# Three-pass products with whole passes, an input projection on raw rows, and branch rows split one per tile

## The chip, the cores and the metric

The kernel runs on one core of a Trainium2 chip. A core has TensorE (PE: matrix products into PSUM banks), VectorE (DVE), ScalarE (ACT), GpSimd (POOL) and SyncE (SP, which mostly issues DMAs). Each engine runs its own list of instructions in order; they wait for one another by semaphores. The metric is the device time of one execution in microseconds, as the median of several runs.

## The reference

One layer of a streaming encoder over T = 1152 tokens (1024 of a prompt and 8 x 16 of samples), width D = 1024. A combined projection of the normalised input feeds three token mixers and their gates; the gated branches are merged and projected, and cross attention and a gated convolutional feed-forward block follow:

```python
def rmsnorm(x, g):
    y = x * rsqrt(mean(x * x, axis=-1) + 1e-6)
    return y * g
...
xn = rmsnorm(x, norm_mix)
lru_x, lru_y, swa, rw, gl = split(xn @ w_in)          # 1024 -> 52 x 128 columns
oA = rg_lru(causal_conv(lru_x)) * gelu(lru_y)
oB = sliding_window_attention(swa)                    # window 128, learned sinks
oC = rwkv7_mix(rw)                                    # token shift, delta rule
gates = sigmoid(gl + b_gate)                          # 3 x 1024
merged = sum(gates[n] * (o @ w_branch[n]) for n, o in enumerate((oA, oB, oC)))
x = x + merged @ w_out
x = x + cross_attention(rmsnorm(x, norm_x), mem_keys, mem_values)
x = x + conv_ffn(rmsnorm(x, norm_ffn))
y = rmsnorm(x, norm_final)
```

The mean of squares is one number per token, so `rmsnorm(x, g) @ W` is also `((x * g) @ W) * rs` with `rs` = 1 / root of the mean square of each token.

## The kernel before

Activations lie transposed: 128 features on the partitions, k = 8 blocks of features, 1152 tokens along the free axis in 3 chunks of 384. The program is a chain of stages with a barrier after each: input projection (`stage_in_projection`, L584), linear recurrence, delta rule, merge (`stage_merge`, L1745, which also computes memory keys and values and the queries), cross attention, and a tail (output of the attention, feed-forward).

Nearly all matmuls belong to a `Product` (L116): y = W x in float32 accuracy from rounded factors. ScalarE rounds a weight tile of 128 output columns, `hi` (`split_hi`, L168), VectorE takes the remainder, `lo` = raw - hi (`split_lo`, L177), and x is split into `xh` and `xl` in the same way. TensorE adds three passes, hi xh, lo xh and hi xl, into one PSUM bank per chunk. Weight tiles alternate between two sets of buffers (s = 0, 1), two tiles are a pair p, and `load_first` and `load_rest` (L143, L149) let SP load a raw tile as soon as its predecessor in the buffer has its remainder taken. `pipeline` (L187) writes out the order on ScalarE and VectorE: the split of a tile, then the evacuation `evac` of the tile before it. `products` (L238) writes out TensorE's: `first_tile` (L262) follows the operands as they come, `tile` (L242) the rest. In `tile`, the three passes are done for k-block 0, then for k-block 1, and so on; ahead of the first matmul stand a wait for `rest` (the remainder of this weight) and one for `used` (the banks evacuated). The function `extra` puts other work, that of the window attention, behind every ninth matmul of sixteen tiles of the input projection.

The input projection first normalises: SP loads the constants (135 KB), the masks (1060 KB), then x in three chunks of columns (1536 KB each), the first two weight tiles behind the first chunk. `Norm` (L311) squares on ScalarE (L343), sums over features by matmuls with a matrix of ones (L366), takes the root on ScalarE (L350) and the reciprocal on VectorE (L373), and then the normalised x is split (up to L390). Of 52 tiles the first 14 are stored as they are, the next 14 are shifted and mixed by VectorE, and the last 24 are gates. ScalarE copies a tile from PSUM (L688) and issues its store; the shifted tiles it copies into padded rows. `PromptWindows` puts the attention within windows beside 16 of the tiles (scores, softmax on VectorE from L542 to L578, transposes on TensorE at L480).

In the merge stage each of the three branches has 4 rows (128 x 1152) as operands and 8 tiles of weights with 4 k-blocks. A `StreamSplit` (L1703) loads rows into a ring of three, rounds them on ScalarE (L1728) and takes the remainder on VectorE (L1732). ScalarE and VectorE do the four rows of branch n + 1 as a block ahead of the pipeline of branch n, with gates (L1851) and splits of weights behind them.

Of the kernel before, what the change touches and what calls it, by code (L numbers as in the profile page):

```python
# [14 lines left out]
F32 = mybir.dt.float32  # L15
F32R = mybir.dt.float32r
ALU = mybir.AluOpType
# [98 lines left out]
class Product:  # L116
# [121 lines left out]
    def products(self, pe, x_rest, by_chunk, beside=None, freed=None, after_row=None, after_tile=None):  # L238
# [3 lines left out]
        def tile(p, s, wait, extra=None, freed=None):  # L242
            pe.wait_ge(self.rest, p * 2 + (s + 1))
            if wait:
                pe.wait_ge(self.used, (p * 2 + (s - 1)) * self.ntc)
            elif self.after:
                pe.wait_ge(self.after.used, 2 * self.after.pairs * self.after.ntc)
            passes = ((self.hi, self.xh), (self.lo, self.xh), (self.hi, self.xl))
            for k in range(self.kt):
                for n, (w, x) in enumerate(passes):  # L250
                    for c in range(self.ntc):
                        last = k == self.kt - 1 and n == 2
                        mm = pe.matmul(self.bank[s][c][:, 0:self.tc], w[s][:, k, :],  # L253
                                       x[:, k, c * self.tc:(c + 1) * self.tc], start=(k == 0 and n == 0), stop=last)
                        if last:
                            mm.then_inc(self.ready, 1)
                if extra:
                    extra(pe, p, s, k)
                if freed and k < self.kt - 1:
                    mm.then_inc(freed, 1)  # L260
# [18 lines left out]
        first_tile()  # L279
        tile(0, 1, False)  # L280
# [303 lines left out]
def stage_in_projection(nc, env, io):  # L584

    with Stage(nc, "inproj") as st:
# [5 lines left out]
        x_in = [st.sem(f"x_arrived{c}") for c in range(NTC)]  # L592
# [5 lines left out]
        norm = Norm(st, "norm", xt, vec[:, VAT["norm_mix"]:], xh, xl, env["mask"]("ones"), banks)  # L598
        norm.eps = env["eps"]
# [12 lines left out]
        with nc.Block() as block:  # L612
            @block.sync
            def _(sp):
                sp.dma_start(vec[:], io["vec"]).then_inc(vec_in, 16)
                sp.dma_start(masks[:], io["masks"]).then_inc(vec_in, 16)
                for c in range(NTC):
                    sp.dma_start(xt[:, :, c * TC:(c + 1) * TC], io["xt"][:, :, c * TC:(c + 1) * TC]).then_inc(x_in[c], 16)
                    if c == 0:
                        prod.load_first(sp)  # L620
# [12 lines left out]
            def _(pool):  # L633
# [3 lines left out]
                pool.wait_ge(norm.rest, NTC * KD)  # L637
# [20 lines left out]
            def _(act):  # L658
                act.wait_ge(eps_set, 2)
                norm.squares(act, x_in, prod)  # L660
                norm.roots(act)

                def shifted(p, s):
                    if after_first(p):
                        act.wait_ge(S(f"shifted{s}"), p * 2 - 2 * R0)
                        act.wait_ge(S(f"z_last{s}"), p - R0)
                        act.wait_ge(S(f"z_last_prompt{s}"), p - R0)
                    else:
                        act.wait_ge(norm.rest, NTC * KD)
                    for c in range(NTC):  # L670
                        act.wait_ge(prod.ready, (p * 2 + s) * NTC + (c + 1))
                        n = TC if c < NTC - 1 else SEQ - c * TC
                        act.copy(zp[s][:, 1 + c * TC:1 + c * TC + n], prod.bank[s][c][:, 0:n]).then_inc(S(f"z_copied{s}"), 1)
                    act.copy(padded(zp[s])[:, :, 1:], prod.bank[s][NTC - 1][:, TC - NB * NS:TC].rearrange("p (b s) -> p b s", b=NB)).then_inc(S(f"z_copied{s}"), 1)
                    act.wait_ge(S(f"z_copied{s}"), p * 4 + (4 - 4 * R0))
                    act.sem_inc(prod.used, NTC)
# [2030 lines left out]
```

## Time and profile before

| | before |
|---|---|
| runs (us) | 2826.38, 2832.47, 2825.57; median 2826.38 |
| profiled execution | 2832.27 us, span 2830.7 us |
| mean granted TensorE clock | 0.949 |
| TensorE busy | 2559.3 us, 90% of the span, 20320 matmuls |
| VectorE busy | 1344.4 us, 47% |
| ScalarE busy | 729.4 us, 26% |
| GpSimd busy | 226.9 us, 8% |
| DMA | 258.92 MB, mean 91 GB/s |

Shares are of the span. An engine's busy time says nothing on what waits for what: that is in the chain of work that ended last and in the table of waits. Times in the rows further down are microseconds from the start of the span.

### The profile page before, as it was taken

The numbers are of one execution on the slowest core, as the hardware profiler recorded it, in microseconds if no ns is written. First come the engines' busy times: TensorE is split into PE (matmuls) and PEld (weight loads), VectorE is DVE, ScalarE is ACT, GpSimd is POOL, SyncE is SP. The second block draws the span as 40 slices with busy tenths as digits, with TensorE's granted clock in tenths as the row PEclk, the third lists the DMA queues.
The fourth block names the chain that finished last, engine by engine and source line by source line (L and its number), as shares of the span: only waits on it lengthen the run. The fifth ranks groups of instructions, "written<-read, shape, count | busy, mean of one in ns | idle before, by whom it ended". The sixth has DMA issues, their size and how long they took to land. (4 is left out here: it accounts for less than half of the span.)

```text
span 2830.7 us, 48844 instructions
## 1 busy us (share of the span) xinstructions
PE 2559.3 (90%) x20320; PEld 2447.7 (86%) x20320; DVE 1344.4 (47%) x2030; ACT 729.4 (26%) x1085; POOL 226.9 (8%) x382
## 2 busy tenths in 40 slices
PE   6999999999657888948999996699999999999996
PEld 4999999999546777838999895599999999999995
DVE  5012334341466777533663513436665555643346
ACT  4111222221344444313332302323111111112122
POOL 0001110000212233200000000000000000000000
PEclk9999999999858999959999998999999999999998
DMA  3222233322630110024441417421111111132233
GB/s 131 82 91 82 91 107 110 108 92 90 138 116 28 33 36 20 14 82 166 141 152 63 147 72 276 142 94 38 45 54 69 57 59 69 69 107 98 72 94 123
DMA packets 138020, 258.92 MB, mean 91 GB/s; under 512 B 43440, under 2 KB 86240, under 8 KB 135056
## 3 DMA queue, kind: packets, MB, share of 16 engines
q1 hardware_dynamic: 103104, 184.25, 20.1%
q0 software_dynamic: 10464, 43.52, 4.5%
q10 hardware_dynamic: 24320, 29.23, 2.9%
q8 instruction: 102, 1.67, 0.3%
q14 instruction: 30, 0.25, 0.0%
HBM read 190.36 MB, written 67.52 MB: 91 GB/s over the span
## 5 line engine op out<-in xcount | busy, mean ns | idle before, releaser
L253 PE MATMUL tail_bank<-tail_x_hi,tail_w_hi 128*128 128x384 f32 x1494 | 359.6, 339 | 8.2 <-DVE tail_w_lo L180 8.2
L253 PE MATMUL tail_bank<-tail_x_lo,tail_w_hi 128*128 128x384 f32 x1494 | 358.3, 339 | 0.0
L253 PE MATMUL tail_bank<-tail_x_hi,tail_w_lo 128*128 128x384 f32 x1494 | 358.2, 339 | 0.0
L253 PE MATMUL inproj_bank<-inproj_xh,inproj_win_hi 128*128 128x384 f32 x1224 | 283.0, 340 | 0.0
L253 PEld LDWEIGHTS tail_bank<-tail_x_hi,tail_w_hi 128*128 128x128 f32 x1494 | 270.7, 188 | 11.8 <-DVE tail_w_lo L180 11.3
L253 PE MATMUL inproj_bank<-inproj_xl,inproj_win_hi 128*128 128x384 f32 x1224 | 278.6, 336 | 0.0
L253 PE MATMUL inproj_bank<-inproj_xh,inproj_win_lo 128*128 128x384 f32 x1224 | 278.5, 336 | 0.0
L253 PEld LDWEIGHTS tail_bank<-tail_x_hi,tail_w_lo 128*128 128x128 f32 x1494 | 270.9, 188 | 0.0
L253 PEld LDWEIGHTS tail_bank<-tail_x_lo,tail_w_hi 128*128 128x128 f32 x1494 | 270.7, 188 | 0.0
L253 PEld LDWEIGHTS inproj_bank<-inproj_xh,inproj_win_hi 128*128 128x128 f32 x1224 | 216.2, 189 | 2.7 <-issue 2.7
L253 PEld LDWEIGHTS inproj_bank<-inproj_xh,inproj_win_lo 128*128 128x128 f32 x1224 | 218.1, 188 | 0.0
L253 PEld LDWEIGHTS inproj_bank<-inproj_xl,inproj_win_hi 128*128 128x128 f32 x1224 | 218.1, 188 | 0.0
L175 ACT CAST tail_w_hi<-tail_w_raw 128x1024 fp32r<-128x1024 f32 (+2 forms) x100 | 92.5, 925 | 474.9 <-PE tail_bank L253 314.0
L253 PE MATMUL merge_bank<-merge_operands,merge_w_hi 128*128 128x384 f32 x840 | 181.9, 340 | 13.5 <-DVE merge_w_lo L180 13.5
L180 DVE TENSOR_TENSOR inproj_win_lo<-inproj_win_raw,inproj_win_hi 128x1024 fp32r<-128x1024 f32 x52 | 63.5, 1223 | 250.0 <-ACT inproj_win_hi L175 250.0
L253 PEld LDWEIGHTS merge_bank<-merge_operands,merge_w_hi 128*128 128x128 f32 x840 | 151.7, 192 | 14.2 <-DVE xt L1932 8.9
L2503 DVE TENSOR_TENSOR tail_room<-tail_bank,tail_rs 128x384 f32<-128x384 f32 x132 | 59.5, 506 | 181.8 <-PE tail_bank L253 181.5
L253 PE MATMUL merge_bank<-merge_operands,merge_w_lo 128*128 128x384 f32 x588 | 135.4, 338 | 0.0
L180 DVE TENSOR_TENSOR tail_w_lo<-tail_w_raw,tail_w_hi 128x1024 fp32r<-128x1024 f32 (+2 forms) x100 | 106.8, 1068 | 54.8 <-ACT tail_w_hi L175 54.7
L1741 DVE TENSOR_TENSOR xt<-tail_bank,xt 128x384 f32<-128x384 f32 x96 | 47.9, 551 | 168.5 <-PE tail_bank L253 155.9
L253 PEld LDWEIGHTS merge_bank<-merge_operands,merge_w_lo 128*128 128x128 f32 x588 | 106.5, 191 | 0.0
L688 ACT COPY inproj_z<-inproj_bank 128x384 f32<-128x384 f32 x114 | 47.6, 497 | 201.9 <-PE inproj_bank L253 201.2
(388 smaller groups left out, 3935.3 us busy)
## 6 DMA issues: line engine op xcount, KB each, us to landing
inproj_win_raw<-in_w_in SPq DMA_DIRECT2D x52, 512.0 KB, 3.6
tail_w_raw<-in_w_up SPq DMA_DIRECT2D x44, 512.0 KB, 4.3
scratch_z<-inproj_z ACTq DMA_DIRECT2D x38, 576.0 KB, 2.8
merge_gate<-scratch_z POOLq DMA_DIRECT2D x24, 576.0 KB, 4.0
scratch_h<-tail_room SPq DMA_DIRECT2D x18, 576.0 KB, 3.1
tail_room<-scratch_h POOLq DMA_DIRECT2D x18, 576.0 KB, 4.6
tail_w_raw<-in_w_down SPq DMA_DIRECT2D x24, 384.0 KB, 3.1
merge_w_raw<-in_w_mem_kv SPq DMA_DIRECT2D x16, 512.0 KB, 3.4
```

The source lines that it names most:

```text
L175: act.copy(self.hi[s][:, 0:self.kt], self.raw[s][:, 0:self.kt]).then_inc(self.rounded, 1)
L180: dve.tensor_tensor(self.lo[s][:, 0:self.kt], self.raw[s][:, 0:self.kt], self.hi[s][:, 0:self.kt].bitcast(F32), ALU.subtract).then_inc(sel ...
L253: mm = pe.matmul(self.bank[s][c][:, 0:self.tc], w[s][:, k, :], x[:, k, c * self.tc:(c + 1) * self.tc], start=(k == 0 and n == 0), stop=last)
L688: act.copy(out[s][:, c * TC:(c + 1) * TC], prod.bank[s][c][:, 0:TC]).then_inc(prod.used, 1)
L1741: dve.tensor_tensor(row, prod.bank[s][c][:, 0:TC], row, ALU.add).then_inc(prod.used, 1)
L2503: dve.tensor_tensor(u[s][:, 2 + c * TC:2 + c * TC + n], up.bank[s][c][:, 0:n], rs[:, c * TC:c * TC + n], ALU.mult).then_inc(S(f"u{s}"), 1)
```

## The change

Three edits, all without a change in what is computed.

1. `tile` does each pass for all k-blocks before the next pass, in the order hi xh, hi xl, lo xh. At its start it waits for `rounded` (the `hi` of this weight); for `rest` (the `lo`) it waits ahead of the first matmul of the third pass. Where rows of x are to be freed one by one (`freed`), the order stays by k-block. The other work (`extra`) still comes behind every ninth matmul.
2. The input projection works on raw x times the gain. x is loaded by rows, w0, x0, w1, x1 to x7, and the masks behind them. ScalarE makes xh (L698 of the new kernel) and squares (L693), VectorE xl (L748) and the sum of squares (L743). TensorE does the first two tiles together, row by row (`first_pair`, L296), then three matmuls with ones on the summed squares (L811). The first two outputs are copied unscaled and multiplied by `rs` in SBUF; of all later tiles VectorE multiplies the banks by `rs` as it evacuates them (L775), and ScalarE only issues the store. `put_sinks` comes behind the first pair.
3. In the merge stage the rows of branches 1 and 2 are handled one per tile of the branch before: in gate i ScalarE issues the load of row i and rounds row i - 1, and VectorE takes the remainder of row i - 1 behind evacuation i.

On TensorE, a tile of the input projection in its first loop stood before as a sequence of threes (`inproj_xh`, `inproj_xl`: the split x; `inproj_win_hi`, `inproj_win_lo`: the split weight tile), twenty-four threes in a tile:

```order
L253 MATMUL inproj_bank<-inproj_xh,inproj_win_hi 128x384 [waits inproj_win_w_rest]
L253 MATMUL inproj_bank<-inproj_xh,inproj_win_hi 128x384 x2
L253 MATMUL inproj_bank<-inproj_xh,inproj_win_lo 128x384 x3
L253 MATMUL inproj_bank<-inproj_xl,inproj_win_hi 128x384 x3
L253 MATMUL inproj_bank<-inproj_xh,inproj_win_hi 128x384 x3
```

and in the changed kernel such a tile, whole, is this (its wait for the rounded weight, `w_rounded`, stands on an instruction ahead of it that only handles the loop's numbers):

```order
L245 ISA [waits inproj_win_w_rounded]
L258 MATMUL inproj_bank<-inproj_xh,inproj_win_hi 128x384 [waits inproj_win_product_used]
L258 MATMUL inproj_bank<-inproj_xh,inproj_win_hi 128x384 x23
L258 MATMUL inproj_bank<-inproj_xl,inproj_win_hi 128x384 x24
L258 MATMUL inproj_bank<-inproj_xh,inproj_win_lo 128x384 [waits inproj_win_w_rest]
L258 MATMUL inproj_bank<-inproj_xh,inproj_win_lo 128x384 x23
```

The wait for the remainder has moved from the first matmul to the forty-ninth, and it is carried by that matmul.

On ScalarE, at the start of the merge stage, the difference reads thus (`merge_operands_9069` and `merge_operands_8918` are the operands of branch 0, `merge_operands` those of branch 1, `merge_branch` the ring of raw rows, L1816 of the new kernel the rounding of a row, L1804 the issue of its load):

```order
 L175 CAST merge_w_hi<-merge_w_raw 128x512 x2
-L1728 CAST merge_operands_9069<-merge_branch 128x1152 x4
-L1728 CAST merge_operands<-merge_branch 128x1152 x4
-L1851 ACT_TABLE_LOAD
-L1851 ACTIVATE merge_gate<-merge_gate,vec 128x1152
-L175 CAST merge_w_hi<-merge_w_raw 128x512
```

```order
+L1816 CAST merge_operands_8918<-merge_branch 128x1152 x4
+L1929 ACT_TABLE_LOAD
+L1929 ACTIVATE merge_gate<-merge_gate,vec 128x1152
+L1804 DMA merge_branch<-scratch_branch 128x1152
+L175 CAST merge_w_hi<-merge_w_raw 128x512
+L1929 ACTIVATE merge_gate<-merge_gate,vec 128x1152
+L1816 CAST merge_operands<-merge_branch 128x1152
+L1804 DMA merge_branch<-scratch_branch 128x1152
+L175 CAST merge_w_hi<-merge_w_raw 128x512
```

Of the eight roundings ahead of the first gate four are left; the others stand one behind each gate, each followed by the issue of the next load.

The diff, cut to its core:

```diff
@@ products
         def tile(p, s, wait, extra=None, freed=None):
-            pe.wait_ge(self.rest, p * 2 + (s + 1))
+            pe.wait_ge(self.rounded, p * 2 + (s + 1))
...
-            passes = ((self.hi, self.xh), (self.lo, self.xh), (self.hi, self.xl))
-            for k in range(self.kt):
-                for n, (w, x) in enumerate(passes):
+            passes = ((self.hi, self.xh), (self.hi, self.xl), (self.lo, self.xh))
+            if freed:
+                steps = [(n, k) for k in range(self.kt) for n in range(3)]
+            else:
+                steps = [(n, k) for n in range(3) for k in range(self.kt)]
+            for i, (n, k) in enumerate(steps):
+                if (n, k) == (2, 0):
+                    pe.wait_ge(self.rest, p * 2 + (s + 1))
...
+        def first_pair():
+            passes = ((self.hi, self.xh), (self.lo, self.xh), (self.hi, self.xl))
+            for k in range(self.kt):
+                pe.wait_ge(x_rest, k + 1)
+                for s in range(2):
+                    if k == 0:
+                        pe.wait_ge(self.rest, s + 1)
...
@@ stage_in_projection, SyncE
-                sp.dma_start(masks[:], io["masks"]).then_inc(vec_in, 16)
-                for c in range(NTC):
-                    sp.dma_start(xt[:, :, c * TC:(c + 1) * TC], io["xt"][:, :, c * TC:(c + 1) * TC]).then_inc(x_in[c], 16)
-                    if c == 0:
-                        prod.load_first(sp)
+                for k in range(KD):
+                    if k < 2:
+                        sp.dma_start(prod.raw[k][:], prod.w(0, k)).then_inc(prod.arrived[k], 16)
+                    sp.dma_start(xt[:, k], io["xt"][:, k]).then_inc(x_in[k], 16)
+                sp.dma_start(masks[:], io["masks"]).then_inc(S("masks_in"), 16)
@@ ScalarE
+                for k in range(KD):
+                    if k < 2:
+                        prod.split_hi(act, 0, k)
+                    act.wait_ge(x_in[k], 16)
+                    act.activation(xh[:, k], xt[:, k], ACT.Identity, scale=gain(k)).then_inc(S("x_rounded"), 1)
+                    if k:
+                        square(k - 1)
+                square(KD - 1)
...
+                def first_pair():
+                    act.wait_ge(S("row_summed"), KD - 1)
+                    for s in range(2):
+                        for c in range(NTC):
+                            act.wait_ge(prod.ready, s * NTC + c + 1)
+                            act.copy(out[s][:, chunk(c)], prod.bank[s][c][:, 0:TC]).then_inc(prod.used, 1)
+                        if s:
+                            break
+                        for c in range(NTC):
+                            act.wait_ge(S("summed"), c + 1)
+                            act.activation(rs[:, chunk(c)], sum_bank(c), ACT.Sqrt, scale=1.0 / D, bias=env["eps"][:, 0:1]).then_inc(S("rooted"), 1)
...
-                    for c in range(NTC):
-                        act.wait_ge(prod.ready, (p * 2 + s) * NTC + (c + 1))
-                        act.copy(out[s][:, c * TC:(c + 1) * TC], prod.bank[s][c][:, 0:TC]).then_inc(prod.used, 1)
                     act.wait_ge(prod.used, (p * 2 + (s + 1)) * NTC)
-                    act.dma_start(io["z"][bass.ds(p * 2 + s, 1)].rearrange("o p t -> (o p) t"), out[s][:]).then_inc(stored[s], 16)
+                    store(p, s)
@@ VectorE
+                        for c in range(NTC):
+                            dve.wait_ge(prod.ready, (p * 2 + s) * NTC + (c + 1))
+                            dve.tensor_tensor(out[s][:, chunk(c)], prod.bank[s][c][:, 0:TC], rs[:, chunk(c)], ALU.mult).then_inc(prod.used, 1)
@@ TensorE
+                def sums():
+                    pe.wait_ge(S("masks_in"), 16)
+                    pe.wait_ge(S("row_summed"), KD - 1)
+                    for c in range(NTC):
+                        if c >= 2:
+                            pe.wait_ge(S("rooted"), c - 1)
+                        pe.matmul(sum_bank(c), env["mask"]("ones"), acc[:, chunk(c)], start=True, stop=True).then_inc(S("summed"), 1)
+                prod.products(pe, S("x_rest"), False, windows, after_pair=sums)
@@ stage_merge, ScalarE
-                    if n < 2:
-                        splits[n + 1].scalar(act)
...
+                        if n < 2:
+                            next_row(splits[n + 1], p * 2 + s)
+                    def next_row(stream, i):
+                        if i == 0:
+                            act.wait_ge(splits[n].rest, KM)
+                            if n:
+                                act.wait_ge(prods[0].ready, KD * NTC)
+                        if 1 <= i <= KM:
+                            stream.scalar_row(act, i - 1)
+                        if i < KM:
+                            stream.load_row(act, i)
@@ VectorE
-                    if n < 2:
-                        splits[n + 1].vector(dve)
...
+                        if n < 2 and 1 <= p * 2 + s <= KM:
+                            splits[n + 1].vector_row(dve, p * 2 + (s - 1))
```

## Rows read from the trace of the kernel before

**Rows 1.** The chain that ended last: start, length, engine, tile, line, count

```profile
1962.46 544.56 PE tail_bank L253 x3094
```

**Rows 2.** Waits of TensorE: waiting line, releaser, total us, times, longest

```profile
PE merge_bank L253 <- DVE merge_w_lo L180: 20.3, 4, 8.6
...
PE tail_bank L253 <- DVE tail_w_lo L180: 14.2, 8, 4.5
...
PE inproj_bank L366 <- ACT inproj_norm_sq L343: 13.7, 3, 13.1
...
PE inproj_bank L273 <- DVE inproj_xl L390: 11.2, 15, 2.8
```

**Rows 3.** Timeline of the start: time, length, engine, line, operation, [wait before]

```profile
11.11 1.28 ACT L343 ACT_TABLE_LOAD   x1 [11.11 <-DMA inproj_xt<-in_xt]
...
23.71 1.28 ACT L350 ACT_TABLE_LOAD   x1
25.01 0.58 ACT L350 ACTIVATE inproj_norm_rs<-inproj_bank,eps 128x384 f32<-128x384 f32 x1
...
64.03 0.68 PE L253 MATMUL inproj_bank<-inproj_xh,inproj_win_hi 128*128 128x384 f32 x3
...
76.52 0.68 PE L253 MATMUL inproj_bank<-inproj_xh,inproj_win_hi 128*128 128x384 f32 x3
```

**Rows 4.** DMA from 0 to 100 us, 40 slices of 2.5 us

```profile
GB/s 29 314 366 405 419 398 401 402 206 272 26 0 0 0 0 0 0 3 0 0 7 3 0 0 0 0 236 129 80 0 0 230 96 126 0 0 236 56 154 0
```

**Rows 5.** Timeline of the merge stage: instructions of 1152 columns

```profile
1543.52 1.17 ACT L1872 ACTIVATE merge_gate<-xt 128x1152 f32<-128x1152 f32 x1
...
1550.58 1.26 ACT L1878 ACTIVATE merge_operands<-xt,vec 128x1152 fp32r<-128x1152 f32 x1
...
1543.40 1.35 DVE L1963 TENSOR_TENSOR merge_branch<-merge_branch,merge_gate 128x1152 f32<-128x1152 f32 x1
...
1552.26 1.41 DVE L1967 SCALAR_TENSOR_TENSOR merge_merged_lo<-xt,vec,merge_operands 128x1152 fp32r<-128x1152 f32 x1
```

**Rows 6.** Timeline of a window tile: ScalarE, VectorE, TensorE

```profile
430.09 1.26 ACT L688 COPY inproj_z<-inproj_bank 128x384 f32<-128x384 f32 x3
...
432.08 1.05 ACT L175 CAST inproj_win_hi<-inproj_win_raw 128x1024 fp32r<-128x1024 f32 x1 [0.72 <-ACT inproj_z L688]
...
431.82 0.49 DVE L542 COPY inproj_attended<-inproj_bank 128x128 f32<-128x128 f32 x2 [6.86 <-PE inproj_bank L459]
433.16 1.22 DVE L180 TENSOR_TENSOR inproj_win_lo<-inproj_win_raw,inproj_win_hi 128x1024 fp32r<-128x1024 f32 x1 [0.85 <-ACT inproj_win_hi L175]
...
438.91 0.69 DVE L578 TENSOR_TENSOR inproj_scores<-inproj_scores,inproj_stat 128x512 f32<-128x512 f32 x1
...
443.56 0.60 PE L480 MATMUL inproj_bank<-masks,inproj_scores 128*128 128x128 f32 x4
```

**Rows 7.** Busy time (PE, PEld, DVE, ACT, POOL), granted clock, DMA share, GB/s of a stretch

```profile
1294.00:1300.30 6.30, 6.17 (x21) 6.18 (x22) 1.99 (x4) 1.31 (x2) 1.05 (x2) 0.57 0.78 264
```

**Rows 8.** Timeline at the memory keys: VectorE's reciprocals, TensorE's wait

```profile
1563.38 7.37 DVE L1991 RECIPROCAL merge_gated<-merge_gated 128x384 f32<-128x384 f32 x3
...
1571.88 0.58 PE L253 MATMUL merge_bank<-merge_mem_hi,merge_w_hi 128*128 128x256 f32 x1 [5.94 <-DVE merge_w_lo L180]
```

**Rows 9.** The page's groups: busy us, mean ns, idle before and releaser

```profile
L2503 DVE TENSOR_TENSOR tail_room<-tail_bank,tail_rs 128x384 f32<-128x384 f32 x132 | 59.5, 506 | 181.8 <-PE tail_bank L253 181.5
...
L180 DVE TENSOR_TENSOR tail_w_lo<-tail_w_raw,tail_w_hi 128x1024 fp32r<-128x1024 f32 (+2 forms) x100 | 106.8, 1068 | 54.8 <-ACT tail_w_hi L175 54.7
```

**Rows 10.** Timeline of the merge stage: TensorE's stalls, ScalarE's rows

```profile
1294.13 1.33 PE L253 MATMUL merge_bank<-merge_operands,merge_w_hi 128*128 128x384 f32 x3 [8.62 <-DVE merge_w_lo L180]
...
1351.70 1.32 PE L253 MATMUL merge_bank<-merge_operands,merge_w_hi 128*128 128x384 f32 x3 [4.91 <-DVE merge_w_lo L180]
...
1281.80 1.16 ACT L1728 CAST merge_operands<-merge_branch 128x1152 fp32r<-128x1152 f32 x1 [5.82 <-DMA merge_branch<-scratch_branch]
...
1303.12 0.62 ACT L175 CAST merge_w_hi<-merge_w_raw 128x512 fp32r<-128x512 f32 x1 [3.27 <-PE merge_bank L253]
```

More of the change, by code:

```diff
@@ L247, in tile @@
                 pe.wait_ge(self.after.used, 2 * self.after.pairs * self.after.ntc)
-            passes = ((self.hi, self.xh), (self.lo, self.xh), (self.hi, self.xl))
-            for k in range(self.kt):
-                for n, (w, x) in enumerate(passes):
[L251 to L260, printed above, removed]
+            passes = ((self.hi, self.xh), (self.hi, self.xl), (self.lo, self.xh))
[6 more added lines that the diff above has]
+                    pe.wait_ge(self.rest, p * 2 + (s + 1))
+                w, x = passes[n]
+                for c in range(self.ntc):
+                    mm = pe.matmul(self.bank[s][c][:, 0:self.tc], w[s][:, k, :],
+                                   x[:, k, c * self.tc:(c + 1) * self.tc], start=(i == 0), stop=(i == len(steps) - 1))
+                    if i == len(steps) - 1:
+                        mm.then_inc(self.ready, 1)
+                if i % 3 == 2:
+                    if extra:
+                        extra(pe, p, s, i // 3)
+                    if freed and k < self.kt - 1:
+                        mm.then_inc(freed, 1)
         def first_tile():
@@ L278, in first_tile @@
                     after_row(k)
-        first_tile()
-        tile(0, 1, False)
+        def first_pair():
[5 more added lines that the diff above has]
+                        pe.wait_ge(self.rest, s + 1)
+                    for n, (w, x) in enumerate(passes):
+                        for c in range(self.ntc):
+                            last = k == self.kt - 1 and n == 2
+                            mm = pe.matmul(self.bank[s][c][:, 0:self.tc], w[s][:, k, :],
+                                           x[:, k, c * self.tc:(c + 1) * self.tc], start=(k == 0 and n == 0), stop=last)
+                            if last:
+                                mm.then_inc(self.ready, 1)
+        if after_pair:
+            first_pair()
+            after_pair()
+        else:
+            first_tile()
+            tile(0, 1, False)
         if after_tile:
@@ L597, in stage_in_projection @@
         vec, masks = env["vec"], env["masks"]
[L598 to L599 removed]
+        gain = lambda k: vec[:, VAT["norm_mix"] + k:VAT["norm_mix"] + k + 1]
+        chunk = lambda c: slice(c * TC, (c + 1) * TC)
+        sum_bank = lambda c: banks[6 + c % 2][:, 0:TC]
         prod = Product(st, "win", KD, Z_N // 2, wtile(io["w_in"], KD), xh, xl, banks)
@@ L686, in evac @@
-                    for c in range(NTC):
-                        act.wait_ge(prod.ready, (p * 2 + s) * NTC + (c + 1))
-                        act.copy(out[s][:, c * TC:(c + 1) * TC], prod.bank[s][c][:, 0:TC]).then_inc(prod.used, 1)
+                    if isinstance(p, int) and p == 0:
+                        first_pair()
+                        return
+                    if isinstance(p, int) and p == 1 and s == 0:
+                        for i in range(2):
+                            act.wait_ge(S("first_scaled"), i + 1)
+                            store(0, i)
@@ L1786, in _ @@
                         splits[0].load(sp)
-                    if n < 2:
-                        if n:
-                            sp.wait_ge(prods[0].ready, KD * NTC)
-                        sp.wait_ge(splits[n].rest, KM)
-                        splits[n + 1].load(sp)
                     prods[n].load_rest(sp)
```

107 lines of the change are left out of this document (66 added, 41 removed).

## The prediction

> **What bounds the kernel now.** I read the page's first section first: TensorE is busy for 90% of the span and no other engine for half of it. The chain of waits then shows whether that is one dense stretch, and it is: one row of it is 3094 matmuls in 544.56 us without a gap, 0.176 us each [rows 1]. There are tile boundaries inside that row, and the tiles before the change take two waits at their start, so a wait whose semaphore is already up costs nothing that the trace shows. In such stretches the change can't gain, since the matmuls keep their number (20,320 less 24 ones-matmuls plus 3). What it can gain stands in the table of what TensorE waits for [rows 2]: 20.3 us before tiles of the merge stage and 14.2 us before tiles of the tail for a weight remainder (`w_lo`), 13.7 us for squares and 11.2 us for rows of `xl` at the start of the input projection. The wait for the very first operands of the merge stage stays as it is: the four rows of branch 0 are still loaded and split as a block, ahead of everything.
>
> **The start, before.** The timeline of the first 80 us [rows 3]: the first chunk of x is there at 11.11, squares, ones-matmuls on them, a first root at 25.01, reciprocals and the normalisation follow, and the first two tiles are done when tile (1,0) starts at 76.52. A tile in full flow is the 12.49 us from 64.03 to 76.52, for 72 matmuls: 0.1735 us each.
>
> **The start, after.** Eight rows of x (576 KB each) come instead of three chunks (1536 KB), and masks (1060 KB) move behind all of them. The slices of 2.5 us in [rows 4] give what had been moved by when: 2731 KB (2.797 MB) ahead of the end of the first chunk are through at 10.0, and it was used at 11.1, so 1.1 us lie between. By the same slices 647 KB (constants, w0) are through at 4.4 and 1223 KB (and x0) at 6.1: w0 is there at 5.5, x0 at 7.2. Then ScalarE multiplies row 0 (1.26, [rows 5]) to 8.5, VectorE takes the remainder (1.41) to 9.9, and TensorE starts at about 10; I take 10.5. The two tiles are 144 matmuls, 144 x 0.1735 = 25.0 us. Is TensorE what bounds them? Per row it needs 18 x 0.1735 = 3.1 us, ScalarE 1.26 + 1.17 = 2.43 (product and square), VectorE 1.41 + 1.35 = 2.76 (remainder and sum), a row of x 576 KB at about 400 GB/s = 1.5 us. So yes, narrowly. For a low clock after the idle start I add 2.5 us, which is what the restart in the merge stage cost (below), at a granted clock of 0.57; the pair then ends at 38. Behind it stand three ones-matmuls, and the third waits for the first root: tile (0,0) is ready 1.6 us before the pair's end; ScalarE then does one weight split (about 1.05), three evacuations (1.26, both [rows 6]), the table load (1.28) and a root (0.58) [rows 3], 4.2 us, so the third ones-matmul starts 2.6 after the pair's end and is through in some 0.5. Tile (1,0) starts at about 42 (41 by the terms, one for the hand-overs): 76.5 - 42 = **34.5 us gained**. Bounds: with the clock up at once 37; with VectorE as the bound and a low clock for the whole pair (6.17 / 21 = 0.294 us a matmul, [rows 7], 42 us) 18. The reciprocals (7.4 us for three, [rows 8]) and the scaling of the first two outputs lie beside tile (1,0) and wait on no one there.
>
> The table load is in the trace 1.28 us, and the root starts 0.02 us behind it [rows 3]. The Trainium skill ("ScalarE: Activation LUTs", section "What ACT_TABLE_LOAD costs") gives a switch 1283 ns of load and some 1380 ns of drain. By that page tile (1,0) would start 1.4 us later and the sum be 1.4 us smaller; the row shows no such drain, and I take the row.
>
> **Other tiles of the projection.** Their evacuation goes from ScalarE copies to VectorE products (0.506 us a chunk for such an instruction, [rows 9]), ScalarE only issues the store once VectorE is done. Outside the window tiles a tile leaves 12.5 us for 1.5 us of evacuation, 1.22 of split and the mixing, so TensorE covers it: 0. In the sixteen window tiles VectorE also has the softmax. In [rows 6] ScalarE ends its evacuation at 431.35, issues the store and begins the split 0.72 us later; VectorE ends the attended copies at 432.31, the weight's remainder at 434.38 and the probabilities at 439.60, and TensorE transposes them at 443.56, so 3.9 us are to spare. After the change VectorE evacuates behind the attended copies, to 432.31 + 3 x 0.506 = 433.8; with 0.72 for the store ScalarE splits from 434.5 to 435.6, and the remainder ends at 436.9: everything moves 2.5 us, and 1.4 are left. I take 0; the other end is in the third rival.
>
> **Pass order.** A tile now waits for `hi` at its start and for the remainder two thirds in, 8.3 us later for k = 8. Where the remainder was late, TensorE starts when `hi` is there. In steady loops nothing was late: 0. The mid-tile wait sits on a matmul, 192 times; as the gapless row says, 0 when up. Bound from the other side in rival two.
>
> **Merge.** TensorE stands 8.62 us at 1294.13 and 4.91 us at 1351.70 [rows 10], because ScalarE and VectorE have four rows of the next branch ahead of the split that this tile needs: 4 x 1.16 us of work on ScalarE, and waits for DMA of up to 5.8 us between them. After each stall the matmuls are slow: the first 21 take 6.17 us at a granted clock of 0.57 [rows 7], so partly at the lower level of 1.2 GHz, against 21 x 0.176 = 3.7 at 2.4 GHz: 2.5 more, and some 2.7 the second time. Now one row a tile: ScalarE has a gate (1.26, as the wide products of [rows 5]), a row (1.16) and a split (0.62, both [rows 10]) in a tile of 36 x 0.1735 = 6.25 us; VectorE has six evacuating instructions of 0.5 us, a row's remainder (1.35) and a split, some 5 us. Rows are issued one tile ahead, so each has about 6 us to land. 8.6 + 2.5 + 4.9 + 2.7 = **18.7 gained**. Lower bound 5: ScalarE now waits for a row's landing with a split queued behind it, so a row later than 6 us holds the next tile. No gain beyond 20, since no more waits are there.
>
> **Memory keys and the tail.** At 1571.88 a tile waits 5.94 us for a remainder that stands behind three reciprocals of 7.37 us on VectorE [rows 8]; `hi` was ready before. The tile's first two passes, 16 matmuls of 256 columns, can now run inside that wait, and the remainder comes as late as ever: 16 x 0.1735 x 256/384 = 1.9 at full clock, 3.1 at the low one; **2** (0 to 4). In the tail 8 waits make 14.2 us; at each TensorE now starts earlier by at most one VectorE split, 1.07 us in the mean [rows 9], and in the longest (4.5) the tile's `hi` was late too. 8 x 1.07 = 8.5 less what is shorter than that: **7** (2 to 12).
>
> **Sum.** 34.5 + 18.7 + 2 + 7 = 62. The profiled execution took 2832.3 us (span 2830.7 and 1.6 around it): 2770. It was 5.9 above the median of the runs, 2826.4, so by the median **2764**.
>
> **Rivals.**
> 1. *Only part comes.* The start goes by the slow clock or by VectorE (gain 18 to 24), and ScalarE's wait for rows keeps half of the merge stalls (9). For it: 2.76 against 3.1 us a row is narrow, and the wait for a branch row in the trace was as long as 5.82 us [rows 10]. Against: those loads were all issued at once, beside each other. 21 + 9 + 1 + 4 = 35: 2791 (2780 to 2800).
> 2. *The mid-tile wait costs.* The matmul that carries it can't be prepared ahead, say 0.1 us on 192 tiles = 19 us: 2783; it takes 62 / 192 = 0.32 us a tile to eat all of the gain. Against: no gap at tile starts with waits of the same kind.
> 3. *Slower: the window tiles.* If the softmax chain on VectorE comes more than 1.4 us later than I moved it, each microsecond costs 16 us over sixteen tiles. To be slower than before by more than the bound below it must overrun by (62 + 8.5) / 16 = 4.4 us a tile; at 5 us it is 80 - 62 = 18 slower, 2844. For it: evacuation, split and store are now in one chain across two engines. Against: three evacuations of 0.5 us and a store's issue don't make 6 us, and ScalarE loses three copies of the same length there.
> 4. *The change doesn't do what it says*: the compiler's order shows the passes whole and the rows one by one, so only the data could be late in the same way again: within 0.3%.
>
> **How the numbers follow.** Forecast 0.66, first rival 0.22, second 0.05 (nearly all of it still faster), third 0.04, fourth 0.03. 0.3% is 8.5 us, about what a measurement of this kernel can tell from no change. Faster: 0.66 + 0.22 + 0.04 = 0.92; within 0.3%: 0.04; slower 0.04. The range: the upper ends of the terms (37 + 20 + 4 + 12 = 73) give 2753, and I put 2750; on the other side it takes in most of the first and second rival: 2790.
>
> **What would show it.** Right: tile (1,0) starts near 42 us; from 10 us on TensorE has no wait of over 1 us but the third ones-matmul; no waits for `w_lo` in the merge stage and none there over 2 us for `w_hi`; waits of the tail near 7 us; the start of the transposes in the window tiles without a wait. Wrong: gaps of 0.1 us or more before the first `lo` matmul of a tile; a new wait of the transposes for the probabilities, sixteen times; a first pair of over 32 us. If the start's gain is above 24 us and the merge waits are gone, and the time is still above 2790, the loss is in the tiles and the second rival is the place to look.

## The result: 67 us faster, five below the forecast

The changed kernel takes 2759.06 us (median of four runs, 2756.87 to 2765.87) against 2826.06 us before (four runs, 2825.57 to 2832.47): ratio 0.9762, 95% interval 0.9739 to 0.9785. The forecast was 2764. The profiled execution took 2756.87 us, its span is 2755.3, and the mean granted clock rose from 0.949 to 0.958.

The page's first section after (busy us, share of the span, instructions) shows the work that moved: VectorE has 69 us more, ScalarE 67 us less, for the evacuations of the projection; TensorE lost 41 us of busy time with just 42 recorded matmuls fewer (each ones-matmul stands twice in the trace, 48 before and 6 after). Of the 41, 15 are the ones-matmuls of the start, 6 lie in the delta rule, whose code is the same, and most of the rest are matmuls that ran slowly before.

```profile
PE 2518.4 (91%) x20278; PEld 2426.8 (88%) x20278; DVE 1413.5 (51%) x2163; ACT 662.5 (24%) x889; POOL 215.9 (8%) x382
```

**Where the 75.4 us between the two profiled executions lie.** From the timelines of TensorE I read the end of each stage's last matmul; a stage is the time between two such ends:

| stage | before | after | difference | forecast |
|---|---|---|---|---|
| input projection | 735.0 | 699.9 | -35.1 | -34.5 |
| linear recurrence (unchanged) | 88.2 | 88.4 | +0.2 | 0 |
| delta rule (unchanged) | 423.7 | 418.7 | -5.0 | 0 |
| merge, with memory keys and queries | 454.1 | 429.6 | -24.5 | -20.7 |
| cross attention (unchanged) | 125.2 | 124.5 | -0.7 | 0 |
| tail | 987.7 | 977.3 | -10.4 | -7 |

The delta rule has the same code in both. In thirteen profiles of this study it took between 418.6 and 425.8 us, cross attention between 122.2 and 128.2: most of the spread from run to run lies there. So 70 us lie in the changed stages, some 5 are chance, and the comparison by medians, 67, is close to the 70.

**The start.** The timeline after (time, length, engine, line, operation, wait before) answers to [rows 3]:

```profile
5.19 1.28 ACT L175 ACT_TABLE_LOAD   x1 [5.19 <-DMA inproj_win_raw<-in_w_in]
...
7.44 1.25 ACT L698 ACTIVATE inproj_xh<-inproj_xt,vec 128x1152 fp32r<-128x1152 f32 x1
...
8.78 1.41 DVE L748 SCALAR_TENSOR_TENSOR inproj_xl<-inproj_xt,vec,inproj_xh 128x1152 fp32r<-128x1152 f32 x1
...
10.25 1.33 PE L296 MATMUL inproj_bank<-inproj_xh,inproj_win_hi 128*128 128x384 f32 x3 [10.25 <-DVE inproj_xl L748]
...
37.48 1.24 ACT L711 COPY inproj_z<-inproj_bank 128x384 f32<-128x384 f32 x3
...
38.73 1.28 ACT L716 ACT_TABLE_LOAD   x1
40.02 1.05 ACT L716 ACTIVATE inproj_rs<-inproj_bank,eps 128x384 f32<-128x384 f32 x2
...
40.66 0.91 PE L811 MATMUL inproj_bank<-inproj_sum_of_squares,masks 128*128 128x384 f32 x2 [1.38 <-ACT inproj_rs L716]
...
41.11 4.62 PE L258 MATMUL inproj_bank<-inproj_xh,inproj_win_hi 128*128 128x384 f32 x24
```

TensorE starts at 10.25 us (forecast 10.5), the pair ends at 37.8 (38), and tile (1,0) starts at 41.11 (42), where it was 76.52. No matmul of the pair waits for a row, once the first is there. The first 18 matmuls are slow, 5.7 us instead of 3.1. After the pair the order is the forecast's: evacuation, table load, root, third ones-matmul behind a wait of 1.38 us. The root starts 0.01 us behind the end of the table load. The Trainium skill ("ScalarE: Activation LUTs", section "What ACT_TABLE_LOAD costs") has a drain of some 1380 ns in such a switch; this row, like that of before, shows none, and the measurement decides.

**The window tiles.** In the same view VectorE's last step of the softmax and TensorE's transposes, which answer to the last two rows of [rows 6]:

```profile
397.12 1.48 DVE L775 TENSOR_TENSOR inproj_z<-inproj_bank,inproj_rs 128x384 f32<-128x384 f32 x3
400.41 1.23 DVE L180 TENSOR_TENSOR inproj_win_lo<-inproj_win_raw,inproj_win_hi 128x1024 fp32r<-128x1024 f32 x1 [1.81 <-ACT inproj_win_hi L175]
...
406.06 0.69 DVE L603 TENSOR_TENSOR inproj_scores<-inproj_scores,inproj_stat 128x512 f32<-128x512 f32 x1
```

```profile
408.45 0.60 PE L505 MATMUL inproj_bank<-masks,inproj_scores 128*128 128x128 f32 x4
```

The probabilities end at 406.75, the transposes start at 408.45 without a wait: 1.70 us to spare, of 3.96 before; the forecast was 1.4.

**The merge stage.** The second pair of branch 0 answers to the first row of [rows 10]: its matmuls follow on the first pair without a wait. ScalarE's first row of the next branch waits 0.72 us for its DMA where it waited up to 5.82.

```profile
1238.09 4.32 PE L258 MATMUL merge_bank<-merge_operands,merge_w_hi 128*128 128x384 f32 x24
...
1244.33 4.32 PE L258 MATMUL merge_bank<-merge_operands,merge_w_hi 128*128 128x384 f32 x24
```

```profile
1240.85 1.16 ACT L1816 CAST merge_operands<-merge_branch 128x1152 fp32r<-128x1152 f32 x1 [0.72 <-DMA merge_branch<-scratch_branch]
...
1244.59 0.62 ACT L175 CAST merge_w_hi<-merge_w_raw 128x512 fp32r<-128x512 f32 x1 [2.58 <-PE merge_bank L258]
```

At the memory keys (to [rows 8]) the tile behind the reciprocals now stops ahead of its last pass instead of its first:

```profile
1510.15 1.56 PE L258 MATMUL merge_bank<-merge_mem_hi,merge_w_lo 128*128 128x256 f32 x8 [4.15 <-DVE merge_w_lo L180]
```

**What TensorE waits for.** The table of waits after (waiting line, releaser, total us, times, longest), for the rows that answer to [rows 2] and those that are new:

```profile
PE inproj_bank L296 <- DVE inproj_xl L748: 10.2, 1, 10.2
...
PE tail_bank L258 <- ACT tail_w_hi L175: 8.3, 5, 4.4
...
PE merge_bank L258 <- DVE merge_w_lo L180: 4.1, 1, 4.1
...
PE inproj_bank L811 <- ACT inproj_rs L716: 1.4, 1, 1.4
...
PE merge_bank L279 <- issue: 0.9, 1, 0.9
```

In the merge stage the 20.3 us of waits for a remainder are down to 4.1, all of it in one tile of the memory keys; the 0.9 is new and stands ahead of the queries. In the tail 14.2 are down to 8.3, and what ends them now is `hi`, not the remainder. The chain that ended last (start, length, engine, tile, line, count) has a long row of the same length, to the hundredth of a microsecond, which answers to [rows 1]:

```profile
1897.21 544.56 PE tail_bank L258 x3094
```

544.56 us for 3094 matmuls, with a wait inside every tile where there was none before.

### The profile page after: what moved, and what is told of

It is laid out like the page before. It is cut to its first block and busy times, and to the rows that moved or that the text cites. A ratio compares the mean times of both kernels' runs of the same rounds, so it can differ in the third digit from the quotient of the medians.

```text
span 2755.3 us, 48597 instructions
## 1 busy us (share of the span) xinstructions
PE 2518.4 (91%) x20278; PEld 2426.8 (88%) x20278; DVE 1413.5 (51%) x2163; ACT 662.5 (24%) x889; POOL 215.9 (8%) x382
## 5 line engine op out<-in xcount | busy, mean ns | idle before, releaser
L258 PE MATMUL tail_bank<-tail_x_hi,tail_w_hi 128*128 128x384 f32 x1494 | 277.2, 338 | 3.9 <-ACT tail_w_hi L175 3.9
L258 PE MATMUL tail_bank<-tail_x_hi,tail_w_lo 128*128 128x384 f32 x1494 | 276.7, 338 | 0.0
L258 PE MATMUL tail_bank<-tail_x_lo,tail_w_hi 128*128 128x384 f32 x1494 | 276.7, 338 | 0.0
L258 PE MATMUL inproj_bank<-inproj_xh,inproj_win_hi 128*128 128x384 f32 x1200 | 226.3, 340 | 0.0
L258 PE MATMUL inproj_bank<-inproj_xh,inproj_win_lo 128*128 128x384 f32 x1200 | 216.2, 336 | 0.0
L258 PE MATMUL inproj_bank<-inproj_xl,inproj_win_hi 128*128 128x384 f32 x1200 | 216.1, 336 | 0.0
L175 ACT CAST inproj_win_hi<-inproj_win_raw 128x1024 fp32r<-128x1024 f32 x52 | 54.7, 1051 | 437.4 <-DVE inproj_z L775 269.8
L258 PE MATMUL merge_bank<-merge_operands,merge_w_hi 128*128 128x384 f32 x840 | 152.6, 335 | 0.0
L775 DVE TENSOR_TENSOR inproj_z<-inproj_bank,inproj_rs 128x384 f32<-128x384 f32 x108 | 53.3, 548 | 152.2 <-PE inproj_bank L258 152.2
L258 PE MATMUL merge_bank<-merge_operands,merge_w_lo 128*128 128x384 f32 x588 | 108.7, 335 | 0.0
```

The lines of the kernel that those rows point to most:

```text
L175: act.copy(self.hi[s][:, 0:self.kt], self.raw[s][:, 0:self.kt]).then_inc(self.rounded, 1)
L775: dve.tensor_tensor(out[s][:, chunk(c)], prod.bank[s][c][:, 0:TC], rs[:, chunk(c)], ALU.mult).then_inc(prod.used, 1)
```

## The experiments

Three theories stand against each other. *Additive*: each of the three edits takes its own stalls away, and costs nothing elsewhere. *Mid-tile wait*: the wait ahead of the third pass costs something on nearly every tile, and the other edits pay for it. *Window tiles*: VectorE's added work is near a bound there. The first four runs do each edit alone and then all three, the next four take single causes, the last three build on what they showed.

**The new order of passes alone**: `products` as changed, `stage_in_projection` and `stage_merge` as before.

```diff
-            pe.wait_ge(self.rest, p * 2 + (s + 1))
+            pe.wait_ge(self.rounded, p * 2 + (s + 1))
...
+                if (n, k) == (2, 0):
+                    pe.wait_ge(self.rest, p * 2 + (s + 1))
```

> The kernel before with the new pass order and the early start alone (projection and merge stage as before). Theory: the tail loses about 10 us and the memory keys about 5, as in the changed kernel, and the two long stalls of the merge stage (8.6 and 4.9 us) shrink by one split of the remainder each, about 1 us, with the slow matmuls behind them still there: 16 to 19 us faster than before, 2808 to 2811. Rival (the mid-tile wait costs): each of the 192 tiles pays, 0.1 us a tile takes 19 us, so no faster than before, and gaps ahead of the first lo matmul show in the steady loops. Second rival (the order itself, not the early start, gives the gain): as fast, but then a tile that starts on the remainder is as fast too, see wait_rest_first.

2814.76 us (ratio 0.9946, 0.9929 to 0.9963): 14 us faster, with an interval of 10 to 20, a little under what was expected. By stages the tail gives 10.7 (987.7 to 977.0) and the merge stage 9.7 (454.1 to 444.4); in the latter the memory keys give 5.0 (58.6 to 53.6, from their first matmul to the end of their last) and the branches 4.5 (172.6 to 168.1). Of these 20 us the unchanged stages took some 4 back in this execution. The mid-tile wait is not seen. But the stalls of the branches stay, under another name:

```profile
1291.77 0.60 ACT L175 CAST merge_w_hi<-merge_w_raw 128x512 fp32r<-128x512 f32 x1
1291.90 1.49 DVE L1960 TENSOR_TENSOR xt<-merge_bank,merge_gate 128x384 f32<-128x384 f32 x3 [1.21 <-ACT merge_gate L1879]
...
1293.44 6.29 PE L258 MATMUL merge_bank<-merge_operands,merge_w_hi 128*128 128x384 f32 x24 [7.70 <-DVE xt L1960]
```

Starting on `hi` shortens the stall from 8.62 to 7.70 us and no more, because the tile needs its banks too. Its `hi` is there at 1292.37; what ends the wait is VectorE's evacuation of the tile that had these banks before, at 1293.39, and that stands behind the block of rows too. The second stall, 4.91 before and 3.37 here, ends on an evacuation as well. The prediction named only the split that the block holds up; the evacuation is held up with it.

**The new projection alone**: `stage_in_projection` as changed, `tile` and `stage_merge` as before.

```diff
+        if after_pair:
+            first_pair()
+            after_pair()
```

> The kernel before with the new input projection alone (tiles by k-block, remainder waited for at the start, branch rows as a block). Theory: tile (1,0) starts at 41 us against 76.5, and nothing later changes: 35 us faster, 2791. Rival (the parts need each other: in the window tiles the softmax behind VectorE's evacuation is late unless tiles start on hi): 20 us or less, with waits of the transposes in the window tiles.

2792.25 us (0.9864, 0.984 to 0.9889): 36.8 us faster. The stage takes 700.3 us in its profile, as with all three edits, so it needs neither of the others.

**One branch row per tile alone**: `stage_merge` as changed, all else as before.

```diff
-                    if n < 2:
-                        splits[n + 1].scalar(act)
...
+                        if n < 2:
+                            next_row(splits[n + 1], p * 2 + s)
```

> The kernel before with one branch row per tile alone. Theory: both stalls of 8.6 and 4.9 us and the slow matmuls behind them go, 18 to 20 us faster, 2806 to 2808; no wait for w_lo in the three branches. Rival (the early start on hi is what removes the stalls): 5 to 9 us, waits for w_lo of 1 to 4 us remain at the tiles with a row.

2809.73 us (0.9937, 0.9912 to 0.9961): 19.3 us faster. The stage falls from 454.1 to 435.3, and its table of waits has only the memory keys left (5.9 the longest):

```profile
PE tail_bank L253 <- DVE tail_w_lo L180: 15.5, 8, 5.8
...
PE merge_bank L253 <- DVE merge_w_lo L180: 6.7, 2, 5.9
```

**All three again**, on the same chip as its parts; no edit.

> The changed kernel itself again, beside its parts. Theory: the parts add up but for some 2 us that passes and branch rows both take from the same two stalls: 2757 to 2762. Rival (the parts need each other): the sum of the three gains is 10 us or more away from this one's.

2760.98 us (0.9756, 0.9732 to 0.978), 68.1 faster. The parts make 14.3 + 36.8 + 19.3 = 70.4. They add up within what the runs can tell; the few microseconds that two of them share in the stalls of the branches (4.5 us of the passes alone, gone when the rows go) are too few to show beside intervals 10 us wide and more.

**The start on the remainder, with whole passes**: separates the early start from the order.

```diff
-            pe.wait_ge(self.rounded, p * 2 + (s + 1))
+            pe.wait_ge(self.rest, p * 2 + (s + 1))
...
-                if (n, k) == (2, 0):
-                    pe.wait_ge(self.rest, p * 2 + (s + 1))
```

> The changed kernel, but every tile again waits for the weight's remainder at its start; the passes stay whole. Theory (the early start gives the gain): the waits for w_lo in the tail and at the memory keys come back, with low clocks behind them, 12 to 15 us slower than the changed kernel, 2771 to 2774; steady loops unchanged. Rival (the order of the passes gives it): as fast as the changed kernel, 2757 to 2762.

2773.62 us (0.9813, 0.9795 to 0.9831): 13 us above the changed kernel's 2760.98 by medians, 16 by the two ratios. The waits of the tail and of the memory keys are back nearly as they were before the change, those of the branches are not:

```profile
PE tail_bank L256 <- DVE tail_w_lo L180: 13.9, 8, 4.2
...
PE merge_bank L256 <- DVE merge_w_lo L180: 7.3, 3, 5.9
```

The tail takes 987.8 us again, the memory keys 60.3. The order of the passes by itself gives nothing; it is what makes room for the early start.

**More work for VectorE in the window tiles**: each evacuation of the last 24 tiles done once more, or twice more (`range(2 ...)` in the second run).

```diff
+                        for i in range(1 if what == "last" else 0):
+                            for c in range(NTC):
+                                dve.wait_ge(prod.ready, (p * 2 + s) * NTC + (c + 1))
+                                dve.tensor_tensor(out[s][:, chunk(c)], prod.bank[s][c][:, 0:TC], rs[:, chunk(c)], ALU.mult).then_inc(S("again"), 1)
+                            dve.wait_ge(S("again"), ...)
```

> The changed kernel with the three evacuations of each of the last 24 tiles of the projection done twice on VectorE (+1.5 us a tile, a wait on itself between). Theory (1.7 us are to spare in the window tiles): the probabilities are ready 0 to 0.2 us ahead of the transposes or just behind them, 0 to 3 us slower than the changed kernel. Rival (a bound nearer than that, since chains of ScalarE and VectorE feed back into the next tile): 10 us or more slower.

> The same, with the evacuations done three times (+3.0 us a tile). Theory: the chain overruns by 1.2 to 1.6 us in 15 or 16 tiles: 18 to 26 us slower than the changed kernel, and the transposes in those tiles wait 1.2 to 1.6 us for VectorE. Rival (slack elsewhere, the next tile's chain starts earlier relative to TensorE): under 8 us.

Once more: 2764.78 us (0.978, 0.9762 to 0.9799), the stage 701.3 against 699.9, the probabilities end 0.2 to 0.3 us ahead of the transposes in all but the first two of the sixteen tiles. Twice more: 2792.41 (0.9872, 0.9848 to 0.9897), 31 us above the changed kernel by medians and so more than the 18 to 26 expected; the stage, at 724.6, is 24.7 longer. The waits stand where they were expected:

```profile
PE inproj_bank L505 <- DVE inproj_scores L603: 18.0, 15, 1.5
```

```profile
412.33 0.66 PE L505 MATMUL inproj_bank<-masks,inproj_scores 128*128 128x128 f32 x4 [1.54 <-DVE inproj_scores L603]
```

The row of 1.54 us is the longest; the fifteen waits make 18.0 us, 1.2 each, and the fifteen tiles together are 23.5 us longer, 1.6 each (from the first tile's transposes to the sixteenth's, 243.0 us against 219.5). The first window tile has 3.5 us to spare and doesn't wait. So the bound of the third rival exists, 1.7 us away, and once over it the overrun, here 1.3 us, is paid in fifteen tiles.

**The masks first again**:

```diff
                 sp.dma_start(vec[:], io["vec"]).then_inc(vec_in, 16)
+                sp.dma_start(masks[:], io["masks"]).then_inc(S("masks_in"), 16)
                 for k in range(KD):
...
-                sp.dma_start(masks[:], io["masks"]).then_inc(S("masks_in"), 16)
```

> The changed kernel with the masks (1060 KB) loaded ahead of the first weight and row of x again. Theory (bytes ahead of the first row set the start): TensorE starts 2.6 to 3.0 us later, at 12.9 to 13.3 us, and tile (1,0) as much later, 43.8 to 44.2. Rival (the queue overlaps transfers so that the order does not matter, or ScalarE's first steps set the start): less than 1 us later.

One run, 2763.93 us. TensorE starts at 13.18 instead of 10.25, tile (1,0) at 44.27 instead of 41.11: 2.9 and 3.2 us for 1060 KB. The start itself varies, from 10.1 to 11.1 us in the other nine profiles with the new projection, so the shift is 2 to 3 us; less than 1, the rival, it is not. The bytes ahead of the first row set the start, as in the sum, as far as one execution can tell.

```profile
13.18 1.33 PE L296 MATMUL inproj_bank<-inproj_xh,inproj_win_hi 128*128 128x384 f32 x3 [13.18 <-DVE inproj_xl L748]
```

**Two kernels built on the changed one.** In the first the reciprocals of the queries' norm are moved behind the memory keys.

```diff
 def beside_mem(p, s):
-                    if i == 5:
-                        for c in range(NTC):
-                            dve.wait_ge(S("rooted"), c + 1)
-                            dve.reciprocal(rs[:, chunk(c)], rs[:, chunk(c)]).then_inc(S("inverse"), 1)
...
 def scale_q(p, s):                                   # first tile of the queries
+                        for c in range(NTC):
+                            dve.wait_ge(S("rooted"), c + 1)
+                            dve.reciprocal(rs[:, chunk(c)], rs[:, chunk(c)]).then_inc(S("inverse"), 1)
```

> The changed kernel with the three reciprocals of VectorE (7.37 us) moved from between two tiles of the memory keys to the first tile of the queries, where VectorE waits for TensorE anyway. Theory (the remainder was late because it stood behind them): the wait of 4.15 us ahead of the third pass goes, and the slow matmuls behind it, about 1.5 us: 5 to 6 us faster than the changed kernel, and the stretch of the memory keys falls from 53.6 to about 48 us. Rival (weights from DMA are as late, since ScalarE waits 7.36 us for one there): 1 us or less.

2753.84 us (0.9737, 0.972 to 0.9753) against 2759.59 (0.9768, 0.9754 to 0.9781) of the changed kernel on the same chip: 5.7 us, and the wait is gone from the table. From the first matmul of the memory keys to the end of their last it is 48.6 us, 54.2 in the changed kernel beside it.

The second has two moves more: ScalarE takes a root of one column before the first pair ends, which loads the table, and rounds rows 0 and 1 of the hidden units both behind tile 1; VectorE takes their remainders there too.

```diff
                 square(KD - 1)
+                act.activation(early[:], env["eps"][:, 0:1], ACT.Sqrt).then_inc(S("early"), 1)
...
-                        if i < stream.n:
-                            stream.scalar_row(act, i)
+                        late = stream is hidden[0]
+                        for k in ((), (0, 1))[i] if late and i < 2 else (i,):
+                            if k < stream.n:
+                                stream.scalar_row(act, k)
```

> The same, and two more moves: ScalarE loads the table of the square root in its idle time before the first pair ends, and the first row of the hidden units that comes from DMA in the down projection is rounded one tile later, behind the split of a weight that TensorE waits 4.45 us for. Theory: tile (1,0) of the projection starts 1.3 us earlier, at about 39.8; the stall of 4.45 us and some 2 us of slow matmuls behind it go: 12 us faster than the changed kernel, 2746 to 2751. Rival (the row is then late for what follows it, and the stall comes one tile later): 6 us faster.

> The changed kernel itself, beside the two kernels built on it, so that they are compared on one chip: 2757 to 2762, as before.

Its profile shows both: from the end of the first pair to tile (1,0) it is 1.9 us (37.95 to 39.88) instead of 3.3 (37.75 to 41.03 in the changed kernel beside it), the 1.3 us expected; and the stall of 4.5 us in the tail is 0.31:

```profile
2461.64 3.88 PE L258 MATMUL tail_bank<-tail_h_hi,tail_w_hi 128*128 128x384 f32 x12 [4.50 <-ACT tail_w_hi L175]
```

```profile
2453.08 2.37 PE L258 MATMUL tail_bank<-tail_h_hi,tail_w_hi 128*128 128x384 f32 x12 [0.31 <-ACT tail_w_hi L175]
```

From the first to the last matmul on the hidden units (`tail_h`) it is 203.0 us, 209.2 in the changed kernel beside it. Its profiled execution is 2748.16 us, but the five runs go from 2748.16 to 2758.51 with a median of 2754.75 (0.9748, 0.9733 to 0.9763). That is faster than the changed kernel beside it by 4.8 us, not by the 12 expected, and not to be told from the first of the two. That the two moves take their stalls away is shown; that they take 6 us off the time is not.

## Why the prediction held, step by step

- **Start, 34.5 forecast, 35.4 measured** (tile (1,0) at 76.52 and 41.11). Every link was within a microsecond: bytes ahead of the first row (masks_first: 2.9 us for 1060 KB), ScalarE's and VectorE's first step, the pair bound by TensorE, the slow first matmuls at 2.6 us for 2.5, the root ahead of the third ones-matmul. The terms gave 41 for tile (1,0), and the microsecond added for hand-overs wasn't needed. The 2.6 is in part luck: in the ten profiles with the new projection between 9 and 19 matmuls run slowly at the start, 1.4 to 2.9 us beyond full flow. The first rival, a start bound by VectorE, didn't come: VectorE took 2.6 us a row against TensorE's 3.1 and ended the last row of `xl` at 27.4, ten microseconds before the pair's end.
- **Branch rows, 18.7 forecast, 20.2 measured** (first operands to first matmul of the output projection, 172.6 and 152.4 us), 19.3 alone. The stalls are 13.9 of it and the slow matmuls 6.3, for 13.5 and 5.2 in the sum; that is just over the 20 given as the most that could come. No tile waited for a row.
- **Memory keys, 2 forecast, 4.9 measured** (58.6 and 53.6 us). This term was mis-sized, and lies above its bound of 4. The wait behind the reciprocals fell by 1.8 us as forecast (5.94 to 4.15), but I read only this one wait. A second of 0.8 us went too, and before the change the remainder was late by a little at five more starts of tiles, where the prediction's "In steady loops nothing was late" doesn't hold. These waits read 0.04 to 0.14 us, too short for the table, but TensorE's matmuls stand 0.3 to 0.4 us further apart there, 2 us in all; one of them before the change (the last matmul of a tile starts at 1582.20, the next tile at 1582.62, behind the remainder):

```profile
1581.35 1.22 DVE L180 TENSOR_TENSOR merge_w_lo<-merge_w_raw,merge_w_hi 128x1024 fp32r<-128x1024 f32 x1
...
1582.20 0.28 PE L253 MATMUL merge_bank<-merge_mem_lo,merge_w_hi 128*128 128x256 f32 x1
...
1582.62 0.38 PE L253 MATMUL merge_bank<-merge_mem_hi,merge_w_hi 128*128 128x256 f32 x1
```

   The slow matmuls behind the long wait cost 2.0 us before and 1.7 after, so they are little of it. The new wait ahead of the queries takes 0.8 of the 4.9 back. One sign of being right, "no waits for `w_lo` in the merge stage", didn't come as written: the 4.15 us are such a wait, and this very term had left it there. With the reciprocals moved the rest of the wait went, so they were its cause.
- **Tail, 7 forecast, 10.4 measured.** The waits fell by 5.9 (14.2 to 8.3), within the term; of the other 4.5 some 4 are slow matmuls behind the stalls: those that took over 0.225 us cost 10.9 us beyond 0.1735 each before and 6.9 after. With the late start put back the tail had 5.6 us more of waits and was 10.5 longer: again nearly as much beside the waits as in them. In the last stretch, before and after (stretch; PE, PEld, DVE, ACT, POOL busy with counts; granted clock, DMA share, GB/s):

```profile
2753.00:2765.00 12.00, 9.49 (x45) 9.17 (x45) 5.78 (x9) 5.41 (x8) 0.00 (x0) 0.86 0.28 70
2786.00:2800.00 14.00, 11.92 (x56) 11.27 (x57) 8.98 (x12) 4.25 (x8) 0.00 (x0) 0.88 0.36 108
```

```profile
2684.00:2698.00 14.00, 12.38 (x69) 12.06 (x70) 9.10 (x12) 6.54 (x11) 0.00 (x0) 1.00 0.30 86
2714.00:2734.00 20.00, 19.36 (x108) 18.87 (x108) 16.19 (x24) 7.84 (x13) 0.00 (x0) 1.00 0.34 102
```

   In these stretches stalls of up to 2.4 us left a granted clock of 0.86 and 0.88 behind them, stalls of up to 1.4 us left 1.00. The length of a stall alone doesn't decide it: in the kernel of the three mends one of 2.62 us at 1790.04 left 1.00.
- **Pass order in steady loops, 0 forecast, 0 measured**: the row of 544.56 us is the same. The second rival is out.
- **Window tiles, 0 forecast with 1.4 us left; 1.7 left.** The third rival's point was not reached; its price, 16 us for each microsecond of overrun, is near what the twice added work cost, 23.5 us for 1.3.
- **Sum.** 62 forecast against 67 by medians and 70 in the changed stages. The forecast of 2764 is 5 us high. The two terms that fell short by most are the tail, where I left out the slow matmuls behind a stall, and the memory keys, where I counted one wait of several.

## What to carry to other kernels

When a stall is taken away, count what runs slowly behind it as well: here that was 6.3 us behind two stalls of 13.5 us in all in the branches, and some 4 us with 5.9 us of shorter waits in the tail. Waits too short for a table add up as well: look at the spacing of the matmuls at the starts of tiles. A wait can be moved to the place where its operand is first used at no cost, as long as the work ahead of it is long enough; and the order of the work is worth changing for that alone, not for itself. Before work is moved to another engine, measure the slack of the tightest tile it lands in, since an overrun is paid in every such tile.

## What was not expected of the hardware

The slow matmuls at the start don't show in the granted clock. From 10.25 us TensorE's first 18 matmuls take 0.32 us each, nearly twice the 0.1735 of full flow, as the first ones behind the stall of the merge stage did [rows 7]; from 15.8 us on they take 0.173:

```profile
13.29 1.16 PE L296 MATMUL inproj_bank<-inproj_xh,inproj_win_hi 128*128 128x384 f32 x3
...
15.99 0.68 PE L296 MATMUL inproj_bank<-inproj_xh,inproj_win_hi 128*128 128x384 f32 x3
```

Yet the column of the granted clock reads 1.00 for the stretch:

```profile
10.20:16.00 5.80, 5.75 (x19) 5.75 (x20) 5.43 (x5) 5.80 (x6) 0.00 (x0) 1.00 1.03 422
```

That 1.00 isn't a reading. The trace's first record of the granted clock begins at 15.75 us, at full clock, and time without a record is counted as full. The matmuls change pace where the first record begins: here at 15.8 us for a record from 15.75, with the masks first at 19.1 for 19.17, with the three mends at 14.1 for 14.05. 384 columns in 0.32 us are 1.2 columns a nanosecond, the lower of the clock's two levels (1.2 and 2.4 GHz). So at the start of a program the durations of the matmuls tell the clock, and the column says nothing until its first record.
